# Prompt attention in a hybrid decoder step: probability rows weighed before the value product, three branches summed in one PSUM bank

## What is computed

```
s_c = einsum('btgqd,bngd->btgqn', qg, ck) * scale          # compressed keys (CMP)
p_c = softmax(where(valid_c, s_c, NEG_INF)) * valid_c
o_c = einsum('btgqn,bngd->btgqd', p_c, cv)
...                                                        # the same with the selected keys (SEL): o_s
...                                                        # and with the last 512 keys (WIN): o_w
o = g[:, :, 0] * o_c + g[:, :, 1] * o_s + g[:, :, 2] * o_w # g = sigmoid gates
```

## Time and profile before

| | us |
|---|---|
| runs, median (lowest to highest) | 2507.45 (2501.72 to 2516.19) |
| profiled execution | 2502.97 |
| its span, first to last instruction | 2501.2 |
| TensorE busy in the span | 2051.5 (82%) |
| VectorE / ScalarE / GpSimd busy | 1369.3 / 1060.0 / 120.0 |
| prompt attention, about | 775 to 1177 |

### The profile page before, as it was taken

The page is one execution under the profiler, slowest core; times in us unless marked ns, Lnnn a source line. Parts: engine busy times, 40 slices in busy tenths (PEclk is TensorE's granted clock), DMA queues, the critical chain, the costliest instruction groups (busy, mean ns, idle before and its releaser), DMA issues. The chain is left out here.

```text
span 2501.2 us, 29798 instructions
## 1 busy us (share of the span) xinstructions
PE 2051.5 (82%) x10870; PEld 1628.4 (65%) x10870; DVE 1369.3 (55%) x2131; ACT 1060.0 (42%) x1609; POOL 120.0 (5%) x119
## 2 busy tenths in 40 slices
PE   6899856898995889987677879949999999996650
PEld 2898646788885778776142645527888888885540
DVE  1533323544432578776400126658989898884437
ACT  4211113333321467664101112126888787873423
POOL 1000000000000000000001000000100000000002
PEclk9899976999975699998768779868999999998875
DMA  8326235333104700000359182218999999987517
GB/s 271 95 70 16 84 111 202 117 128 113 58 5 87 228 23 17 5 5 17 129 164 225 33 299 89 77 48 320 425 426 415 415 416 411 415 335 275 194 52 287
DMA packets 168247, 444.13 MB, mean 178 GB/s; under 512 B 49157, under 2 KB 96227, under 8 KB 136397
## 3 DMA queue, kind: packets, MB, share of 16 engines
q1 hardware_dynamic: 148589, 340.91, 38.6%
q0 software_dynamic: 14240, 82.99, 10.4%
q10 hardware_dynamic: 5328, 19.02, 1.9%
HBM read 388.32 MB, written 58.77 MB: 179 GB/s over the span
## 5 line engine op out<-in xcount | busy, mean ns | idle before, releaser
L2626 DVE TENSOR_TENSOR moe_lo<-wts_raw,moe_hi 128x2048 fp32r<-128x2048 f32 x216 | 484.4, 2287 | 59.8 <-ACT moe_hi L2541 59.7
L2541 ACT ACTIVATE moe_hi<-wts_raw 128x2048 fp32r<-128x2048 f32 x216 | 401.3, 1915 | 25.2 <-PE moe_U L2423 25.2
L911 PE MATMUL cmp_hp<-cmp_xh,cmp_wh 128*128 128x256 f32 (+1 forms) x576 | 177.0, 307 | 16.5 <-DVE cmp_xl L838 16.5
L911 PE MATMUL cmp_hp<-cmp_xh,cmp_wl 128*128 128x256 f32 (+1 forms) x576 | 174.0, 302 | 0.0
L911 PE MATMUL cmp_hp<-cmp_xl,cmp_wh 128*128 128x256 f32 (+1 forms) x576 | 173.9, 302 | 0.0
L2409 PE MATMUL moe_G<-moe_hi,moe_xh 128*128 128x512 f32 x288 | 117.6, 408 | 44.0 <-DVE moe_lo L2626 36.3
L2449 PE MATMUL moe_Y<-moe_hi,moe_hh 128*128 128x512 f32 x288 | 118.6, 412 | 29.4 <-DVE moe_hl L2642 24.9
L911 PEld LDWEIGHTS cmp_hp<-cmp_xh,cmp_wh 128*128 128x128 f32 x576 | 122.9, 213 | 21.8 <-issue 19.2
L1309 ACT ACTIVATE att_prow<-att_S,att_low 128x640 f32<-128x640 f32 (+15 forms) x192 | 107.7, 563 | 46.5 <-DVE att_low L1367 43.8
L1299 ACT ACTIVATE att_ph<-att_pT 128x512 fp32r<-128x512 f32 (+5 forms) x148 | 88.3, 597 | 87.1 <-PE att_pT L1207 86.8
L911 PEld LDWEIGHTS cmp_hp<-cmp_xh,cmp_wl 128*128 128x128 f32 x576 | 123.1, 214 | 0.0
(11 more groups left out here) (430 smaller groups left out, 4545.0 us busy)
## 6 DMA issues: line engine op xcount, KB each, us to landing
wts_raw<-in_w_gate SPq DMA_DIRECT2D x72, 1024.0 KB, 6.8
wts_raw<-in_w_up SPq DMA_DIRECT2D x72, 1024.0 KB, 7.6
wts_raw<-in_w_down SPq DMA_DIRECT2D x72, 1024.0 KB, 8.2
s_yb<-moe_y ACTq DMA_DIRECT2D x36, 512.0 KB
smp_wa<-in_w_ada SPq DMA_DIRECT2D x8, 2048.0 KB
fro_wraw<-in_w_ada SPq DMA_DIRECT2D x4, 2048.0 KB, 23.3
s_yb<-att_zero SPq DMA_DIRECT2D x1, 8192.0 KB
fro_wraw<-in_w_in SPq DMA_DIRECT2D x12, 512.0 KB, 6.7
```

The costliest lines, as they stand in the source:

```text
L911: last = pe.matmul(hp[k % 2][:, r, 0:cols], lhs[:, w, :], rhs[:, k, t, 0:cols], start=(t == 0 and m == 0), stop=(t == 7 and m == 2))
L2541: act.activation(hi[p][half][:, :], raw[p][half][:, :], ACT.Copy).then_inc(hi_ready[p], 1)
L2626: dve.tensor_tensor(lo[p][half][:, :], raw[p][half][:, :], hi[p][half][:, :], ALU.subtract).then_inc(lo_ready[p], 1)
```

## The change

- Groups are ordered (i, g, branch) with CMP, SEL, WIN inside a g. `LAG` is 4 in place of 2.
- Once a group's four sums are there, VectorE's `weigh` forms gate / sum (a reciprocal and a multiply), and GpSimd, which had nothing in this stage, multiplies the group's four rows of `prow` in place. Only then are they transposed. `prow` is one buffer for each branch.
- The three branches of one (i, g), a pair, then accumulate in one PSUM bank (`op`, two of them). `keep`, `back` and `combine` come once for a pair. `back` is 4 transposes, and `combine` is one reduce that adds the two halves. `fold`, `ob` and `part` go.
- Keys, values and gates come in two loads of whole row pieces (2144 bytes of each position) in place of eleven loads. Key transposes take both g at once, ScalarE and VectorE then work on 64 partitions for each g, and the values are split in halves.
- `sample.load` and the zeros are issued after the loads of the queries of rows 2 and 3, ahead of the store of row 0.

The core of the diff:

```diff
-    NB_S, NPT, LAG = 4, 3, 2
-    groups = [(i, br, g) for i in range(NT) for br in (CMP, SEL, WIN) for g in range(NG)]
+    NB_S, NPT, LAG = 4, 3, 4
+    groups = [(i, br, g) for i in range(NT) for g in range(NG) for br in (CMP, SEL, WIN)]
...
+        tiles += [(grp, j, br == CMP and j == 0, br == WIN and j == n - 1) for j in range(n)]
...
+        if x % QG == 0 and 0 < x <= len(units):
+            order.append(("scale", x // QG - 1))
...
-            for br in range(2):
-                for g in range(NG):
-                    at = SO + 256 * br + g * HD
-                    for c in range(2):
-                        sp.dma_start(zk[:, :, br, g, c * HD:(c + 1) * HD],
-                                     a["s_z"][0:T, at:at + HD].rearrange("(t p) d -> p t d", p=P)).then_inc(k_in, 16)
-            for br in range(2):
-                at = SO + 256 * br + 128
-                sp.dma_start(zv[:, :, br, :, :].rearrange("p t g d -> p t (g d)"),
-                             a["s_z"][0:T, at:at + 128].rearrange("(t p) n -> p t n", p=P)).then_inc(kv_in, 16)
-            sp.dma_start(gate[:, :, :], a["s_z"][0:T, GO:GO + 24].rearrange("(t p) n -> p t n", p=P)).then_inc(kv_in, 16)
+            for half in range(2):
+                sp.dma_start(z[:, 4 * half:4 * half + 4, :],
+                             a["s_z"][512 * half:512 * half + 512, SO:GO + 24].rearrange("(t p) n -> p t n", p=P)).then_inc(z_in[half], 16)
             load_q(1)
-            sample.load(nc, a, sp)
-            sp.dma_start(a["s_yb"][NE * P:NBLK * P, :].rearrange("(p r) (c n) -> p (r c) n", p=P, n=P),
-                         zero[:, :].rearrange("p (o n) -> p o n", o=1).to_broadcast([P, NOV * D // P, P])).then_inc(yb_out, 16)
             for i in range(NT):
                 if i + 2 < NT:
                     sp.wait_ge(ring_full, ring_at[("q", i, 1)] + 1)
                     load_q(i + 2)
+                if i == 1:
+                    sample.load(nc, a, sp)
+                    sp.dma_start(a["s_yb"][NE * P:NBLK * P, :].rearrange("(p r) (c n) -> p (r c) n", p=P, n=P),
+                                 zero[:, :].rearrange("p (o n) -> p o n", o=1).to_broadcast([P, NOV * D // P, P])).then_inc(yb_out, 16)
                 if i >= 1:
...
-                    if first:
-                        pe.wait_ge(exp_done, QG * grp + QG)
+                    br = groups[grp][1]
+                    pe.wait_ge(scaled, grp + 1)
                     for h in range(QG):
-                        last = pe.transpose(dst[0:rows, h, :], prow[grp % 2][:, h, j * P:j * P + rows], ident[:, :])
+                        last = pe.transpose(dst[0:rows, h, :], prow[br][:, h, j * P:j * P + rows], ident[:, :])
...
-                if first and grp:
-                    pe.wait_ge(ot_ready, grp)
+                if br == CMP:
+                    pe.wait_ge(v_ready, 1)
+                else:
+                    pe.wait_ge(v_ready, 2 + br + 2 * (i // 4))
+                if first and grp >= 6:
+                    pe.wait_ge(acc_done, grp // 3 - 1)
+                out = op[grp // 3 % 2]
                 block_ = row_keys(i, br)[0] // P + j
                 lhs = cvv[0:rows, g, :] if br == CMP else vv[:, block_, br, g, :]
-                pe.matmul(op[:, :, :], lhs, ph[n % NPT][0:rows, :, :], start=first, stop=False)
-                pe.matmul(op[:, :, :], lhs, pl[n % NPT][0:rows, :, :], start=False, stop=final).then_inc(pv_done, 1)
-
-            def back(grp):
-                pe.wait_ge(ot_ready, grp + 1)
-                if grp:
-                    pe.wait_ge(ob_free, grp)
+                pe.matmul(out[:, :, :], lhs, ph[n % NPT][0:rows, :, :], start=first, stop=False)
+                pe.matmul(out[:, :, :], lhs, pl[n % NPT][0:rows, :, :], start=False, stop=final).then_inc(pv_done, 1)
+
+            def back(pair):
+                pe.wait_ge(ot_ready, pair + 1)
                 for h in range(QG):
-                    last = pe.matmul(ob[:, h, :], ot[grp % 2][:, h, :], fold[:, :], start=True, stop=True)
-                last.then_inc(ob_full, 1)
+                    last = pe.transpose(op[pair % 2][:, h, :], ot[pair % 2][:, h, :], ident[:, :])
+                last.then_inc(back_done, 1)
...
+        @block.gpsimd
+        def _(pool):
+            for grp, (i, br, g) in enumerate(groups):
+                width = row_keys(i, br)[1]
+                pool.wait_ge(scale_ready, grp + 1)
+                for h in range(QG):
+                    row = prow[br][:, h, 0:width]
+                    last = pool.tensor_scalar(row, row, scale[:, grp, h:h + 1], None, ALU.mult)
+                last.then_inc(scaled, 1)
...
+                dve.wait_ge(exp_done, QG * grp + QG)
+                dve.wait_ge(z_in[i // 4], 16)
+                sums, sc = den[:, grp, :], scale[:, grp, :]
+                if br == CMP and i == 0:
+                    step(dve.tensor_scalar(sums, sums, 1e-30, None, ALU.max))
+                step(dve.reciprocal(sc, sums))
+                dve.tensor_tensor(sc, sc, w, ALU.mult).then_inc(scale_ready, 1)
+
+            def combine(pair):
+                i, g = pair // NG, pair % NG
+                dve.wait_ge(back_done, pair + 1)
+                if i >= 2 and g == 0:
+                    dve.wait_ge(att_out[i % 2], 16 * (i // 2))
+                dve.tensor_reduce(acc[i % 2][:, g * QG:(g + 1) * QG, :],
+                                  op[pair % 2][:, :, :].rearrange("p h (c d) -> p h d c", c=2), AX, ALU.add).then_inc(acc_done, 1)
```

More of the change, by code:

```diff
@@ L1005, in stage_prompt_attention @@
         tiles_of.append(range(len(tiles), len(tiles) + n))
-        tiles += [(grp, j, j == 0, j == n - 1) for j in range(n)]
+        tiles += [(grp, j, br == CMP and j == 0, br == WIN and j == n - 1) for j in range(n)]
     bank_of, bank_after, at, last = [], [], 0, [-1] * NB_S
@@ L1036, in values @@
         if tiles[n][3]:
-            backs.append(tiles[n][0])
+            backs.append(tiles[n][0] // 3)
     backs = []
@@ L1045, in stage_prompt_attention @@
             i, br, g = groups[grp]
[L1046 to L1049 removed]
+            if h == 0 and g == 0 and br != CMP and i in (0, 2):
+                put(("k", br, i // 2))
             if br == SEL and g == 1 and h < 2 and i + 1 < NT:
@@ L1088, in stage_prompt_attention @@
         den = s.sb("den", [P, len(groups), QG])
-        scale = s.sb("scale", [P, QG, 1])
-        prow = [s.sb(f"prow{i}", [P, QG, T]) for i in range(2)]
+        scale = s.sb("scale", [P, len(groups), QG])
+        prow = [s.sb(f"prow{br}", [P, QG, n]) for br, n in ((SEL, T), (WIN, 5 * P), (CMP, T // 16))]
         ph = [s.sb(f"ph{i}", [P, QG, P], F32R) for i in range(NPT)]
@@ L1098, in stage_prompt_attention @@
         pT = [s.ps(f"pT{i}", [P, QG, P]) for i in range(2)]
-        op = s.ps("op", [P, QG, P])
-        ob = s.ps("ob", [P, QG, HD])
+        op = [s.ps(f"op{i}", [P, QG, P]) for i in range(2)]
+        gate = z[:, :, GO - SO:]
         eyer, diagr, farr, cmaskr = maskr[:, 0:P], maskr[:, P:2 * P], maskr[:, 2 * P:3 * P], maskr[:, 3 * P:]
         k_in = s.sem("k_in")
-        kv_in = s.sem("kv_in")
+        z_in = [s.sem(f"z_in{i}") for i in range(2)]
         c_in = s.sem("c_in")
@@ L1282, in high @@
                 if ring[r][0] == "k":
-                    _, br, g, half = ring[r]
+                    _, br, half = ring[r]
                     act.wait_ge(ring_full, r + 1)
-                    act.activation(kT[br][:, g, half * 512:(half + 1) * 512], src[:, :, :].rearrange("p t n -> p (t n)"), ACT.Copy
-                                   ).then_inc(ring_high, 1)
+                    for g in range(NG):
+                        mine = slice(g * HD, (g + 1) * HD)
+                        last = act.activation(kT[br][mine, g, half * 512:(half + 1) * 512],
+                                              src[mine, :, :].rearrange("p t n -> p (t n)"), ACT.Copy)
+                    last.then_inc(ring_high, 1)
                 elif ring[r][0] == "q":
```

108 lines of the change are left out of this document (39 added, 69 removed).

## The result

The changed kernel takes 2605.9 us in the median (2601.8 to 2611.7, 4 runs) against 2511.0 us for the kernel before in the same session. The ratio is 1.038, 95% interval 1.035 to 1.041: 3.8% slower, 95 us. The forecast was 2461 us.

What follows compares the result with a forecast made beforehand. TensorE was taken as nearest to the bound, VectorE close. Start -14, row 0 -7 and rows 1 to 7 -25 make -46: 2457, with 4.5 us from profiled execution to median 2461 us; range 2433 to 2520.

Steps and rivals of the forecast that it cites:

- the price of the pass: GpSimd multiply of one head's row: VectorE's minimum row, 0.82 us at 640 and 1.23 at 1024; upper bound twice that.
- three stretches of row 4: Last SEL score to first SEL tile 5.8 us, on to first WIN tile 7.8, the rest 8.8: 22.4 per head group.
- The slow rival: GpSimd pass takes twice VectorE's row and shows whole in every SEL and WIN group: 85 us more, 2546; chance 0.18.
- the hidden case: GpSimd pass well under VectorE's row, or VectorE's lag overestimated: 30 us less in all, 2431 us; chance 0.15.
- The rival's break-even: GpSimd pass length from which the change turns slower: 1.54 times VectorE's row, 1.27 us for 640 columns.
- The start: Two loads in place of eleven bring the stage's first exponential to 787: -14 us, bounds -11 and -15.
- The rest of the change: Start -14 us, row 0 -7, rows 1 to 7 -25, and 30 us less with GpSimd hidden.
- cold longer: TensorE's clock stays at the 1.2 GHz level through row 1: +10 us, 2471; chance 0.12.
- No wait for the store: Row 0's store, behind sample loads and zeros, lands before row 2's first pair reduces: cover 13 us, cost 0.
- nowhere hidden: Argument for the slow rival: each group's four GpSimd passes and a queue hop between engines are fully exposed.

Runs made afterwards that it cites:

- x13: Changed kernel with GpSimd weighing each group by one `tensor_tensor` in place of four `tensor_scalar`: 2510.7 us, ratio 0.998, stage 411.2 us.
- x1: Changed kernel without the GpSimd multiplies, weighing left out: stage 344.8 us against 495.2, kernel 2495.3 us.
- x4: Kernel before with only the two row loads of keys, values and gates in place of eleven: ratio 0.997, stage 394.3 us.
- x7: Kernel before with the two row loads, and sample loads and zeros behind the queries of rows 2 and 3: ratio 0.994, stage 391.3 us.
- x12: Changed kernel with passes shared over GpSimd, VectorE and ScalarE, plus two useless matmuls ahead of each tile's transposes in rows 0 to 2: 2480.5 us, ratio 0.985.
- x16: Changed kernel, SEL and WIN heads 0 and 1 on VectorE, 2 on ScalarE, 3 and CMP on GpSimd in `tensor_tensor` form: 2508.1 us, ratio 0.996.
- x19: Changed kernel with passes shared over GpSimd, VectorE and ScalarE, plus GpSimd products on its own buffers beside VectorE's passes: VectorE's pass 67 ns longer at 640 columns.

## Why the prediction failed

**The step that failed is the price of the pass.** "I choose VectorE's row, since a multiply by a column scalar reads one operand, as the minimum does": 0.82 us at 640 columns. It measured 1.883, 2.3 times as much and beyond the upper bound of twice the row. It was the one term of the sum that no row of the trace before bore on, and it stood in the middle of its bounds. The number of operands was no guide: with two operands GpSimd is faster (1.255 at 640, 1.893 at 1024), and VectorE does the same one-operand multiply in 0.549. The 1.96 of the Trainium skill (GPSIMD Engine Reference, "Elementwise") is nearer to what happened than its "roughly line rate" for one input, which the trace contradicts: the one-input form is 3.4 times VectorE's time here (1.883 to 0.549). For two inputs these runs show less than the page: 1.893 at 1024 columns against VectorE's 1.225 for a `tensor_tensor` in SBUF, 1.5 times.

**The structure was right, the sizes partly by luck.** With 7.5 us for four passes in place of 3.3, the prediction's three stretches of row 4 become 10.0, 12.0 and 8.8 us, 61.6 for the row; it measured 64.5. In the trace the stretches of one head group are 10.4, 13.9 and 8.8 us (first SEL tile at 983.55, first WIN tile at 997.48, last SEL score ended at 1006.3, next SEL tile at 1016.71). The middle one is 1.9 us over, and it runs mostly at the lower level of the clock (0.57), right behind the stand of 4.13 us (983.5 to 997.4, then 997.4 to 1006.3):

```profile
983.50:997.40 13.90, 12.23 (x46) 10.20 (x46) 5.09 (x12) 5.18 (x14) 7.46 (x4) 0.57 0.05 19
997.40:1006.30 8.90, 8.75 (x58) 7.48 (x58) 6.60 (x12) 6.27 (x14) 1.45 (x4) 1.00 0.31 61
```

There four transposes take 1.1 us in place of 0.62, VectorE comes late to the `weigh` of WIN (989.4), and GpSimd starts late. The prediction reckoned all of this at full clock. With x13's 4.45 the stretches give 6.95, 8.95 and 8.8, 49.4; measured 52.6.

The slow rival named place and mechanism. Its own formula, 85 us for each VectorE row above one, gives 110 us at 2.3 and a sum of +64 us, against +94 measured in the stage. The 30 us between have two parts. From the hidden case (2431 against 2507, -76) to +64 the formula gives the GpSimd chain 140 us, and x1 shows 150. The rest of the change was to bring 76 us and brought 56.5. That the 140 came so close is partly luck: TensorE's waits for GpSimd are only 103.3 us, not 140, and about 58 us of slower matmuls, which the formula doesn't have, stand in their place. By rows the formula is off both ways: row 1 took 31.7 us against 38.7, row 7 took 105.6 against 90.8.

The rival's break-even, 1.54 times the row (1.27 us), came out high: x13's 1.11 us a head (4.454 over 4) is already even with before (median 5 us under, stage 10 us over).

**The start:** first exponential 10.0 us after the identity's issue in place of 25.8: 16 us, forecast 14. Taken alone it was worth 10 us in x4 and 14 in x7 by the medians, 7 and 10 by the stage. So whether a part of it is given back in rows 1 and 2, as the stage has it, stays open.

**The rest of the change:** forecast -76 us with GpSimd hidden, and x1 shows -56.5. Rows 0, 1 and 3 of x1 take 28.4, 28.7 and 35.5 us against 32, 30 and 38.1 in the forecast; row 2 takes 41.4 against 32. Row 2 is half of the 19.5 us that are missing. It ran at 0.71, which looks like the rival "cold longer" one row later, but x12 raised the clock of that row and did not shorten it. Why row 2 is long stays open.

**No wait for the store:** the store of row 0 was issued at 835.36, right behind the zeros, and VectorE has no wait for it, as forecast:

```profile
832.40 1.43 SPq L1164 DMA_DIRECT2D s_yb<-att_zero  x1
835.36 27.88 SPq L1143 DMA_DIRECT2D s_attn<-att_acc  x1
```

**The chance** of 0.18 for slower rested on "nowhere hidden" being weighed against "one operand, and no other work on GpSimd". Neither of the last two bears on the duration of an instruction that no row shows.

## What to carry over

An operation on an engine that the trace never shows doing such work is the widest term of the sum: take its price from one run of it before building an order around it, in each form that the language offers, since one `tensor_tensor` for four rows took 4.45 us where four `tensor_scalar` took 7.46. When a new step stands in a chain between engines, write its duration against the distance that the order of work gives it: at four units of distance 150 us showed, at six and with the better form the same step on the same engine left a kernel 1.7% faster than before. And before work is spread over VectorE and GpSimd at once, look whether VectorE's instruction is one that stands while GpSimd runs: its `tensor_scalar` in SBUF did (0.55 us became 1.65), its reads of PSUM did not.

## What the runs showed of the hardware

- GpSimd, fp32 in SBUF, 128 partitions: `tensor_scalar` 1.883 us at 640 and 2.843 at 1024 columns, 1.812 and 2.772 with a constant; `tensor_tensor` with a broadcast operand 1.255 and 1.893, 7.013 at 4096.
- VectorE's SBUF to SBUF `tensor_scalar` takes 0.549 us at 640 columns, two thirds of a minimum over the same width from PSUM (0.82), and in x16 stops for the length of a GpSimd pass less 0.17 us. In x19 a GpSimd product stops instead (0.75 us in place of 0.39).
- TensorE's granted clock in 860 to 1120: 0.99 before, 0.77 with the stalls, 0.85 with matmuls of no use in them. The same 1760 matmuls of the stage kept TensorE busy 357 us at a mean of 0.75 and 299 at 0.89.
